# Encoder layer on one core: branch C rewritten as a pipeline of tile steps, with four smaller moves in branch A, the merges and the tail

## The reference, cut to what matters

```python
def mixer_layer(x, p_i, ...):
    h = rms_norm(x, pre_g)
    u = h @ w_in
    aq, ak, av, ag, bq, bk, bv, bg, cq, ck, cv, cg, mg = jnp.split(u, split_points, axis=-1)
    ya = diff_attention(aq, ak, av, lam, ...) * jax.nn.silu(ag)      # 4 heads, two softmax maps each
    yb = gqa_attention(rope(rms_norm(bq)), rope(rms_norm(bk)), bv) * jax.nn.silu(bg)
    yc = neighbourhood_attention(cq, ck, cv, rpb) * jax.nn.silu(cg)  # 8 heads, 8 rows x 16 columns
    gates = jax.nn.sigmoid(mg).reshape(b, s, 3, D_MODEL)
    m = gates[:, :, 0] * (ya @ wa) + gates[:, :, 1] * (yb @ wb) + gates[:, :, 2] * (yc @ wc)
    x = x + rms_norm(m @ w_out, post_g)
    return x + jax.nn.sigmoid(x @ w_pg) * (p_i @ w_pe)
```

## Time and profile before

| | us | share of the span | instructions |
|---|---|---|---|
| median of 3 runs | 1512.39 | | |
| the profiled execution, and its span | 1514.99 and 1513.2 | | 18374 |
| TensorE matmul busy | 1400.8 | 93% | 6780 |
| TensorE weight loads | 1132.8 | 75% | 6780 |
| VectorE busy | 607.8 | 40% | 1089 |
| ScalarE busy | 542.7 | 36% | 1000 |
| GpSimd busy | 290.9 | 19% | 180 |

### The profile page before, as it was taken

One profiled execution on the slowest core, in us unless ns is written; L12 is line 12 of the kernel. 1 busy time (PEld: TensorE's weight loads), 2 busy tenths in 40 slices (PEclk: granted clock), 3 DMA queues, 4 the chain that ended last, 5 costly groups with the idle time before them and its releaser, 6 DMA issues.

```text
span 1513.2 us, 18374 instructions
## 1 busy us (share of the span) xinstructions
PE 1400.8 (93%) x6780; PEld 1132.8 (75%) x6780; DVE 607.8 (40%) x1089; ACT 542.7 (36%) x1000; POOL 290.9 (19%) x180
## 2 busy tenths in 40 slices
PE   4999999889999798987999898989898999899998
PEld 3787777678887575765788786878787888788887
DVE  4355555556100636456212115162525212544332
ACT  4354454443111536445211115252524212324432
POOL 1221112212222113020022131211211112213100
PEclk9999999999999999999999999999999999999999
DMA  4211101101111000000011110111100113322200
GB/s 172 71 36 37 45 28 50 45 29 45 42 43 55 28 14 28 14 14 8 22 42 57 61 56 16 54 34 35 34 28 29 42 42 139 112 83 71 69 35 35
DMA packets 25753, 71.87 MB, mean 47 GB/s; under 512 B 2872, under 2 KB 4792, under 8 KB 25568
## 3 DMA queue, kind: packets, MB, share of 16 engines
q1 hardware_dynamic: 25696, 71.09, 14.5%
HBM read 66.86 MB, written 4.23 MB: 47 GB/s over the span
## 4 chain that ended last, share of the span: by engine, by line
PE 71%; DVE 5%; ACT 2%; issue 2%; POOL 0%; DVEq 0%; ACTq 0%
PE ps L639 34%; PE ps L906 9%; PE ps L701 6%; PE ps L1098 6%; PE ps L1080 6%; PE ps L686 3%; PE ps L679 2%; PE ps L658 2%; PE ps L666 2%; PE ps L1104 1%; ACT s L1166 1%; DVE pt_lo L1580 1%; ACT pt_hi L1178 0%; DVE s L1635 0%; DVE s L1610 0%
## 5 line engine op out<-in xcount | busy, mean ns | idle before, releaser
L492 POOL TENSOR_TENSOR w_lo<-stage,w_hi 128x1024 fp32r<-128x1024 f32 (+1 forms) x92 | 193.2, 2100 | 864.2 <-ACT w_hi L1151 863.9
L639 PE MATMUL ps<-h_hi,w_hi 128*128 128x512 f32 x768 | 243.4, 398 | 2.0 <-ACT s L1166 1.8
L639 PE MATMUL ps<-h_lo,w_hi 128*128 128x512 f32 x768 | 237.8, 391 | 0.0
L639 PE MATMUL ps<-h_hi,w_lo 128*128 128x512 f32 x768 | 237.3, 390 | 0.0
L1151 ACT CAST w_hi<-stage 128x1024 fp32r<-128x1024 f32 (+1 forms) x92 | 86.0, 935 | 310.9 <-PE ps L639 222.1
L639 PEld LDWEIGHTS ps<-h_lo,w_hi 128*128 128x128 f32 x768 | 144.7, 188 | 31.0
L639 PEld LDWEIGHTS ps<-h_hi,w_hi 128*128 128x128 f32 x768 | 140.1, 188 | 36.8 <-issue 8.8
L639 PEld LDWEIGHTS ps<-h_hi,w_lo 128*128 128x128 f32 x768 | 144.4, 188 | 30.8
L1580 DVE TENSOR_TENSOR pt_lo<-ps,pt_hi 128x512 fp32r<-128x512 f32 (+2 forms) x160 | 91.3, 603 | 105.2 <-ACT pt_hi L1178 99.1
L658 PE MATMUL ps<-h_hi,w_hi 128*128 128x512 f32 x272 | 113.1, 416 | 0.0
L658 PE MATMUL ps<-h_lo,w_hi 128*128 128x512 f32 x272 | 108.5, 399 | 0.0
(11 more groups left out here) (214 smaller groups left out, 2394.7 us busy)
## 6 DMA issues: line engine op xcount, KB each, us to landing
stage<-in_w_gates SPq DMA_DIRECT2D x24, 512.0 KB, 3.3
stage<-in_w_qkvg_a SPq DMA_DIRECT2D x19, 512.0 KB, 6.0
stage<-in_w_qkvg_c SPq DMA_DIRECT2D x16, 512.0 KB, 3.3
stage<-in_w_branch SPq DMA_DIRECT2D x24, 256.0 KB, 2.6
m<-in_x_tok SPq DMA_DIRECT2D x4, 1024.0 KB, 11.1
y<-in_x_tok SPq DMA_DIRECT2D x8, 512.0 KB, 3.5
stage<-in_w_pg SPq DMA_DIRECT2D x16, 256.0 KB, 2.7
out<-y SPq DMA_DIRECT2D x16, 256.0 KB, 2.0
```

The lines of the kernel that those rows point to most:

```text
L492: nc.gpsimd.tensor_tensor(dst, stage[:, slot, 0:width], f32(hi), ALU.subtract).then_inc(w_ready, 1)
L639: done = mm(ps[:, bank + g, :], w[:, slot, k * P:(k + 1) * P], h[:, k, g * SEQ:(g + 1) * SEQ], start=first and part == 0, stop=last and pa ...
```

## The change

1. **C becomes a line of 32 tile steps** (`step_c` on TensorE, ScalarE and VectorE). Projections come in halves of 512 tokens (`project_pieces`), eight chunks to a step, for the next unit; in the last unit's last six steps (`C_END`) they are the two gate blocks of merge 2, cut into 8, 5, 3, 4, 4, 3 and 5 chunks. In a step TensorE runs one chunk, the turn of head 0, three chunks, the turn of head 1, four chunks; both turns use bank 0. The scores of two tiles are taken together every second step. A mix is 24 matmuls in bank 1: the first covers all 512 columns, for which a corner of `pt_hi` must be zero; GpSimd clears it once, after the last product of merge 1 (`block_done`), ahead of the first two weight splits of C.
2. **The bias of C** is spread in three parts, each as soon as the last tile that uses the old one is done, from two raw buffers (one in a new tile `spare`, which also takes the plain values and the first gate of merge 2).
3. **A**: the diagonal, the spread and the norm of four tiles move from step 2 (6) to step 3 (7) for TensorE's spread and `norm_y`; on VectorE the diagonal stays in step 2 (6), behind the half's low part and the next tile's maximum instead of ahead of them. ScalarE's weight split in A no longer waits for `block_done`.
4. **Merges**: product 6 goes to banks 0 and 1, and product 7 waits for product 5's sum, not 6's.
5. **Tail**: a written-out order of the 16 half tiles (`EMBEDS`), in which six tiles of x2 stay split until their second half, and each tile of x2 is turned once, straight from `m`; `copy_x2` goes.

The core of the diff, by engine:

```diff
+KEPT = 6
+EMBEDS = [(t, 0) for t in range(KEPT)] + [(0, 1), (1, 1), (6, 0), (6, 1), (7, 0), (7, 1)] \
+    + [(t, 1) for t in range(2, KEPT)]
+C_END = {2: [("m0", 0, 0, KC)], 3: [("m0", 1, 0, 5)], 4: [("m0", 1, 5, KC)], 5: [("m1", 0, 0, 4)],
+         6: [("m1", 0, 4, KC)], 7: [("m1", 1, 0, 3)], 8: [("m1", 1, 3, KC)]}
...
 # GpSimd, ahead of C
+            pool.wait_ge(block_done, LEAD + N_C)
+            nc.gpsimd.memset(f32(pt_hi[:, 0, 1, 3 * P:QT * P]), 0.0).then_inc(pt_zeroed, 1)
+            for n in range(2):
+                split_w(N_C + n, n)
+            for part in range(3):
+                spread_bias_c(0, part)
...
 # TensorE
-                if t == 6 or t == 2 and i:
-                    spread_rstd(2 * i if t == 6 else 2 * i - 1)
+                if t == 7 or t == 3 and i:
+                    spread_rstd(2 * i if t == 7 else 2 * i - 1)
...
+            def mix_c(c):
+                todo = [(0, 1, 0, QT, v_hi, pt_hi), (0, 1, 0, 3, v_hi, pt_lo), (0, 1, 0, 3, v_lo, pt_hi)]
+                todo += [(e, k, q0, q1, v, p) for e in range(2) for k, q0, q1 in [(1, 0, 3), (2, 1, 4), (0, 0, 2), (3, 2, 4)]
+                         if (e, k) != (0, 1) for v, p in ((v_hi, pt_hi), (v_hi, pt_lo), (v_lo, pt_hi))]
...
+            def step_c(T):
+                i, t = divmod(T, TILES)
+                pieces = pieces_c(T)
+                project_pieces(T, pieces[:1])
+                if T >= 0:
+                    if t == 4 or t == 0 and i > 0:
+                        mix_c(2 * i if t == 4 else 2 * i - 1)
+                    turn_c(T, 0)
+                project_pieces(T, pieces[1:len(pieces) // 2])
+                name, unit, g = half_of_c(T - 1)
+                if name == "v":
+                    turn_values_c(T - 1, 2 * unit + g)
+                if T >= 0:
+                    turn_c(T, 1)
+                project_pieces(T, pieces[len(pieces) // 2:])
...
             def merge_branch(b, f, n, slot):
-                pe.wait_ge(merged, LEAD + b * KC + f)
+                if isinstance(f, int) and f == KC - 1:
+                    pe.wait_ge(merged, LEAD + b * KC + KC - 2)
+                elif branch_bank(f):
+                    pe.wait_ge(merged, LEAD + b * KC + f)
+                else:
+                    pe.wait_ge(merged, LEAD + b * KC + 1)
...
+            for T in range(TILES_C):
+                if T % 2 == 0 and T + 2 < TILES_C:
+                    score_pair_c(T + 2)
+                step_c(T)
...
 # ScalarE
+            def step_c(T):
+                probs_hi_c(T, 0)
+                if t in (1, 2) or t in (5, 6) and i < UNITS - 1:
+                    split_c(N_C + 4 * i + 4 + [1, 2, 5, 6].index(t))
+                probs_hi_c(T, 1)
+                if half_of_c(T - 1)[0] == "v":
+                    values_hi_c(T - 1)
+                if T + 2 < TILES_C:
+                    exp_c(T + 2)
+                half_out_c(T)
+                if T + 2 < TILES_C:
+                    scale_c(T + 2)
...
 # VectorE
-                if t % 4 == 2 and c >= 0:
-                    make_diagonal(c)
                 half_lo(T - 1)
                 if T + 2 < TILES_A:
                     max_a(T + 2)
+                if t % 4 == 2 and c >= 0:
+                    make_diagonal(c)
...
-                if t % 4 == 2 and c >= 0:
+                if t % 4 == 3 and c >= 0:
                     norm_y(c)
...
+            def step_c(T):
+                if t == 4 or t == 0 and i:
+                    take_y_c(2 * i if t == 4 else 2 * i - 1)
+                probs_lo_c(T, 0)
+                probs_lo_c(T, 1)
+                if half_of_c(T - 1)[0] == "v":
+                    values_lo_c(T - 1)
+                if T + 2 < TILES_C:
+                    max_c(T + 2)
+                    scales_c(T + 2)
+                    norm_c(T + 2)
+                half_lo_c(T)
```

More of the change, by code:

```diff
@@ L573, in _ @@
             split_w(N_MERGE[1] + 15, 1, width=512)
[L576 to L594, removed]
@@ L617, in _ @@
                 out_tile(TILES // 2 - 1, c, c == 1)
[L618 to L622, removed]
+            for k in range(KC):
+                cols = slice(k * 512, (k + 1) * 512)
+                split_w(N_PG[1] + k, k % 2, dst=pg_parts[1][1][:, cols], width=512, hi=pg_parts[1][0][:, cols])
         @block.tensor
@@ new lines, in project_pieces @@
+            def project_pieces(T, pieces):
+                for name, unit, g, bank, k in pieces:
+                    if k == 0:
+                        start_half_c(T, name, unit, g)
+                    slot = 1 if name in ("k", "g", "m1") else 0
+                    for part, (w, h) in enumerate([(w_hi, h_hi), (w_hi, h_lo), (w_lo, h_hi)]):
+                        done = mm(ps[:, bank, :], w[:, slot, k * P:(k + 1) * P], h[:, k, g * SEQ:(g + 1) * SEQ],
+                                  start=k == 0 and part == 0, stop=k == KC - 1 and part == 2)
+                    if k == KC - 1:
+                        done.then_inc(half_done, 1)
@@ L1641, in probs_lo @@
[L1641 to L1646 removed]
+                nc.vector.reciprocal(st[:, 6:8], st[:, 4:6]).then_inc(scales_ready, 1)
@@ L1924, in _, with max_c @@
                 step_a(T)
+            def max_c(T):
+                i, t = divmod(T, TILES)
+                lo, hi = C_KEYS[t % QT]
+                width, first = (hi - lo) * P, C_BIAS[t % QT]
+                if t in (0, 1, 3):
+                    dve.wait_ge(bias_ready, LEAD + UNITS + 3 * i + [0, 1, 3].index(t) + 1)
+                dve.wait_ge(scores, LEAD + BEFORE_C + T + 1)
+                dve.wait_ge(p_turned, LEAD + BEFORE_C + T - 1)
+                dve.sem_inc(dve_entered, 1)
+                st = stat[:, T % 2, :]
+                for e in range(2):
+                    done = nc.vector.tensor_tensor_reduce(
+                        out=s[:, T % 2, e, 0:width], in0=ps[:, 2 + 2 * (T % 2) + e, 0:width],
+                        in1=bias[:, e, first:first + width], scale=1.0, scalar=NEG, op0=ALU.add, op1=ALU.max,
+                        accum_out=st[:, e:e + 1])
+                steps.done(dve, done)
+                nc.vector.tensor_scalar(st[:, 2:4], st[:, 0:2], -1.0, None, ALU.mult).then_inc(maxed, 1)
```

844 lines of the change are left out of this document (459 added, 385 removed).

## The result

The changed kernel takes **1439.76 us** (median; 1439.09 to 1440.64) against 1512.45 us for the kernel before beside it: ratio 0.952, 95% interval 0.9504 to 0.9537, 72.7 us less. The forecast was 1454 us, 1440 to 1476. So the direction was right, the gain was 14 us larger than forecast, and the time lies 0.24 us under the low end of the range. The profiled execution took 1439.09 us, its span 1437.1; between the two profiled spans lie 76.1 us, since the profiled execution of before was 2.5 us over its median and this one 0.7 under.

What follows compares the result with a forecast made beforehand. TensorE, busy nearly everywhere, was taken to bound the kernel. Savings of 27.6 + 1.6 + 7.2 - 4.5 + 19.5 + 0.3 + 7.0 = 58.7 us off the 1512.39 us median gave 1454 us, range 1440 to 1476.

Steps and rivals of the forecast that it cites:

- A: Branch A: spreading the norm one step later ends seven waits and their clock loss, less 1 us given back: 27.6 us saved.
- Merge ends: Ends of the three merges: product 7 waits for merge 5 instead of 6, saving 1.6, 7.2 and 0.3 us.
- Entry of C: Before C's first projection: TensorE newly waits 2.85 us for GpSimd's clear and split, plus 1.7 us clock loss: -4.5 us.
- C itself: Branch C: 270.6 us of work plus waits, clock loss and refills come to 290 against 309.5 us: 19.5 us saved.
- The odd tile: Odd tiles of C: the high half comes 0 to 0.3 us late in ScalarE's queue, costing 2.6 us in all.
- The meetings of negate and split: C: some 3 of 16 VectorE negates meet a GpSimd split, at half a split's 2.39 us: 3.6 us lost.
- The clock behind the last unit's waits: C's last unit: lower clock behind its 7.5 us of waits, costing 4 us.
- Tail: Tail: x2 tiles turned once, so eight turns of 0.87 us leave the chain that sets the end: 7.0 us saved.
- rival 4: C's last unit: its waits are hidden, 11.5 us less, giving 1442 us; chance 0.07.
- rival 1: C: ScalarE's in-order queue makes every odd tile wait 1.15 us, giving 1476 us; chance 0.2.
- rival 2: Branch A: the wait only moves to mix_a, so A's part saves nothing, giving 1482 us; chance 0.05.
- rival 3: C: GpSimd operations stand before the negate in nearly each tile, 32 tiles losing 77 us, giving 1531 us; chance 0.04.

Runs made afterwards that it cites:

- 30.0 alone: The kernel before with only the branch A part of the change: 1483.54 us, 30.0 us less than the kernel before beside it.
- experiment 2: The kernel before with only the branch A part, but VectorE still making the diagonal first in its step: 1490.79 us.
- experiment 3: The changed kernel with the old bank and the old waits for product 6's sum in all three merges: 1447.26 us.
- experiment 5: The changed kernel with GpSimd splitting C's first weight block before it waits for merge 1's last product and clears the corner: 1437.15 us.
- experiment 9: The changed kernel with one more 512-column ScalarE copy in 13 odd steps of C, ahead of the half projection's way out: 1441.29 us.
- experiment 7: The changed kernel with one more split-sized GpSimd operation right behind each of 12 weight splits of C: 1445.69 us.
- experiment 8: The changed kernel with 12 more split-sized GpSimd operations in C, each waiting for VectorE's scaling of head 0: 1439.29 us.
- experiment 11: The changed kernel with five x2 tiles turned a second time in the tail, results unused: 1445.06 us.
- experiment 10: The changed kernel with GpSimd's two halves of w_out waiting for VectorE's low half of the first output tile, VectorE's order kept: 1437.35 us.
- experiment 4: The changed kernel with ScalarE's weight cast in a step of C moved behind the second high half: 1461.98 us.
- experiment 6: The changed kernel with VectorE's order at merge 2's end turned, GpSimd's w_out halves after the first tile's low half, TensorE waiting by chunk: 1435.17 us.

## Why the prediction fell short, step by step

**A: mechanism right, size short.** All seven waits went; 27.6 us were forecast, 30.9 came in the traces and 30.0 alone. The term that was too small is the loss beside the waits: I took the mean granted clock, 0.03 of 295.7 us, for 8.9 us; 30.9 less the 19.7 of waits are 11.2, and by that much TensorE's busy time in A fell (286.90 to 275.71 us in the table's stage). And the 1 us that I gave back did not come, since VectorE's new order (experiment 2, 5.7 us of stage A) keeps the late diagonal out of the next tiles' way.

**Merge ends: right.** 1.6 and 7.2 us were forecast, 1.7 and 7.2 came. Of the 7.2, 2.8 already go with GpSimd's split, which moved out of merge 1 (experiment 3 keeps them with the old bank); the forecast saw only what that move costs at the entry of C. In merge 2 the wait went to the first output tile, as forecast (4.3 us, forecast 4.2), and the stage gained nothing.

**Entry of C: right.** A wait of 2.7 us (forecast 2.85) in the place that was named, and a clock of 0.98 over 68.8 us, 1.4 us by the rounded clock and 2.0 by experiment 5 (forecast 1.7):

```profile
831.12 0.20 POOL L647 MEMSET pt_hi<- 128x128 f32 x1 [8.86 <-PE ps L1028]
831.28 5.67 POOL L540 TENSOR_TENSOR w_lo<-stage,w_hi 128x1024 fp32r<-128x1024 f32 x2
```

**C itself: work right, waits too many. This is the step that failed.** 290 us were forecast, 281.0 came (833.78 to 1114.80). The work of 270.6 us holds: 281.0 less 7.1 of idle time and 2.8 of lower clock (0.02 of 68.84 and 0.03 of 48.80) are 271.1. The last unit's waits were forecast at 7.5 us and came at 6.7. Three terms failed, and a fourth, the refills (1.5 us), had been counted twice, since they are in the 271.1 us of work already. The four make up 10.2 of the 10.7 us by which C with its entry saved more than forecast:

- *The odd tile, 2.6 us.* It has no wait before the last unit. In the step walked through here, TensorE turns head 0 of an odd tile, ScalarE takes its high half 0.95 us later, VectorE the low half, and the second turn comes 0.85 us after that. The walk had it 0 to 0.3 us late. The high half is late in ScalarE's queue, 0.46 us behind the turn's landing (940.43), but that was charged as TensorE's wait, though 0.85 us are left up to the consumer. In the odd tiles ahead of the last unit's waits the high half is 0.23 to 0.49 us late and 0.36 to 1.05 us are left. That is read from the trace alone, since experiment 9 delayed no high half.

```profile
939.94 0.49 PE L932 MATMUL ps<-ident,s 128*128 128x128 f32 x3
...
942.80 0.49 PE L932 MATMUL ps<-ident,s 128*128 128x128 f32 x3
```
```profile
940.89 0.46 ACT L1437 CAST pt_hi<-ps 128x384 fp32r<-128x384 f32 x1
```
```profile
941.39 0.56 DVE L1736 TENSOR_TENSOR pt_lo<-ps,pt_hi 128x384 fp32r<-128x384 f32 x1 [0.73 <-ACT pt_hi L1437]
```

- *The meetings of negate and split, 3.6 us.* I counted them by chance, a fifth of sixteen. In a line of equal steps nothing falls by chance: ScalarE's cast has one place in the step, so GpSimd's split has one too, and here it ends 0.3 to 1 us before the negate (splits from 942.38 to 944.77 and from 949.97 to 952.38; negates at 945.74 and 952.66):

```profile
942.38 2.39 POOL L540 TENSOR_TENSOR w_lo<-stage,w_hi 128x1024 fp32r<-128x1024 f32 x1 [20.23 <-ACT w_hi L1275]
...
949.97 2.41 POOL L540 TENSOR_TENSOR w_lo<-stage,w_hi 128x1024 fp32r<-128x1024 f32 x1 [5.20 <-ACT w_hi L1275]
```
```profile
945.74 0.17 DVE L2043 TENSOR_SCALAR stat<-stat 128x2 f32<-128x2 f32 x1
...
952.66 0.17 DVE L2043 TENSOR_SCALAR stat<-stat 128x2 f32<-128x2 f32 x1
```

  In the whole of C only three negates are drawn out, to 0.43 us, and TensorE waits for none. Experiments 7 and 8 show it both ways. It was in the diff to be read: the cast stands between the two high halves, 2 us ahead of the negate.

- *The clock behind the last unit's waits, 4 us.* It cost 1.5 (0.03 of 48.80 us), and less in other executions: between C's last two mixes, where most of these waits lie, the changed kernel takes 23.3 us, and eight of the nine kernels that keep these steps 21.8 to 22.1.

**Tail: right.** 7.0 us forecast, 7.3 measured, and experiment 11 gives 0.87 us for a turn.

**B and the start** were forecast at no change, and no change can be told from the runs. Of the table's 2.1 and 1.3 us, most of B's lies in the first projection behind the same wait of 2.45 us, where 18 matmuls took 5.93 us before and 4.31 after, but also 6.58 in experiment 10, which has the changed kernel's B.

**The range** failed in its low end, by 0.24 us, which is less than the spread of single executions. It was set by rival 4 (1442) and the forecast's own low end, but the bounds that the text gives for single terms were not added up: A at 29 and C at 35 alone would have reached 1437. All open terms that turned out wrong were costs put on top of a sound sum of work, so the error had one sign.

**The rivals.** Rivals 1 to 3 did not happen; rival 3's mechanism is real (experiments 4 and 7), but in the changed kernel the splits end before the negate. Rival 4 gave 1442, near the result, by luck: the last unit's waits, which it takes away, are all there (6.7 us).

The Trainium skill ("SBUF — State Buffer", section "SBUF: two separate sides") says that the shared port pair is held for a whole instruction by whichever of the two engines begins first, and that on VectorE it concerns its two-port modes and operations with two SBUF inputs. The traces agree on both: the operation with two such inputs took 3.23 us beside a split that had begun 0.20 us earlier and 1.08 without (the difference, 2.15, is about what was left of that split at 2.39 us), and the low halves, which read one input from the bank, kept their mean of 556 ns beside experiment 8's extra operations.

## What to carry to other kernels

In a pipeline of equal steps, place each side engine's operation on the timeline of one step and see what it ends before; its share of the time says nothing of what it meets. Walk the step with measured durations up to the time at which the consumer really asks, and charge only what lies behind that. Add the low bounds of the single terms up when setting a range, since terms that are all costs err together. Before a stage's gain is given to an edit, compare the stage in several profiles that share its instructions.

## What the runs showed of the hardware that I had not expected

The same wait of TensorE is followed by the lower clock in some executions and not in others. Behind B's wait of 2.45 us the same 18 matmuls ran at a mean granted clock of 0.71 in the kernel before, 1.00 in the changed one and 0.63 in experiment 10, which has the same B (chains of work, in this order):

```profile
498.66 5.93 PE ps L639 x18
```
```profile
464.80 4.31 PE ps L704 x18
```
```profile
465.86 6.58 PE ps L705 x18
```

So two profiles of this program can lie some us apart in a stage that the edit does not touch (B took 239.8 to 243.8). Why the clock falls behind the wait in one execution and not in another stays open.

A GpSimd operation is drawn out by VectorE as well. Two splits elsewhere take 2 x 2.39 us; the two halves of w_out took 5.66 beside the first tile's low half in the changed kernel, and 6.65 in experiment 6, beside VectorE's own halves of w_out:

```profile
1224.34 5.66 POOL L540 TENSOR_TENSOR h_lo<-stage,h_hi 128x1024 fp32r<-128x1024 f32 x2 [9.53 <-ACT h_hi L1275]
```
```profile
1221.56 6.65 POOL L540 TENSOR_TENSOR h_lo<-stage,h_hi 128x1024 fp32r<-128x1024 f32 x2 [8.15 <-DVE q_lo L2245]
```
